# A weight ring of three places in place of four, and two and a half weight pieces kept

## The chip, the cores and the metric

One Trainium2 chip, one of its cores. The time is what the device takes for one execution, in microseconds (us), median of the runs shown; lower is better. All data is float32. A megabyte of weights (1024 KB) is one "piece" here, a tile of 128 partitions by 2048 values.

## The reference, cut to what matters

One inference step of a two-layer decoder trunk: 256 prompt tokens and 32 sample tokens (8 sequences of 4), width 1024. Per layer three mixers (a spatial-gating MLP, a gated causal convolution, and cross-attention into 256 memory tokens) share one input projection; then comes a retrieval of single-neuron experts, 8 heads of 16 out of 16384 per token.

```python
xn = _rmsnorm(x, w['norm_mix_g'])
h = xn @ w['w_in']                       # 1024 x 8192, columns split below
u_a, v_a, val_b, gate_b, q_m, gl_a, gl_b, gl_m = jnp.split(h, SPLITS, axis=-1)
y_a, vn = _spatial_gate(gelu(u_a), gelu(v_a), ...)
c = causal_depthwise(val_b * sigmoid(gate_b))
y_b = silu(layernorm(c))
y_m = _mem_attend(q_m, mem_k, mem_v)
merged = sigmoid(gl_a)*(y_a @ w_o_a) + sigmoid(gl_b)*(y_b @ w_o_b) + sigmoid(gl_m)*(y_m @ w_o_m)
x = x + merged @ w_out
# then the retrieval: top 16 of 16 x 16 product keys, per head
hid = gelu(einsum('bd,bhkd->bhk', xb, u_tab[eid]))
x = x + einsum('bhk,bhkd->bd', g * hid, v_tab[eid])
```

The "v half" of the title is v_a: its 1024 x 1024 weights come as four pieces, va 0 to va 3, of 256 columns each.

## The kernel before, in words

**Portions.** The work is cut into four portions. Portions 0 and 2 (even, layers 0 and 1) carry 128 prompt tokens; portions 1 and 3 (odd, same layers) carry the other 128 prompt tokens and the 32 sample tokens. Each portion has a mixing part (dense matmuls with streamed weights) and a retrieval part. The mixing of portion m + 1 runs woven into the retrieval of portion m; the mixing of portion 0 runs alone, at the start, with no gathers beside it.

**Retrieval.** A portion has 8 or 10 steps of 8 units t. A unit gathers 2 x 128 rows of 8 KB of the expert table: POOL issues two indirect DMAs of 1 MB each into one of 5 slots (`gather`, L560), DVE takes dot products with them (L1558), ACT scales (L944), and PE multiplies the value halves (`values`, L2294), which frees the slot (semaphore `v_used`). POOL issues the gather of unit t + 5 when unit t is through.

**Streamed weights.** `items(m)` lists the pieces in the order in which PE wants them. Even portions: glu 0 to 7, mk and q mixed, mv 0, q 3, mv 1 to 3, va 0 to 3, 24 pieces mg mixed with ua 0 to 3, out 0 to 3, wq 0 to 3. Odd portions: glu, q, va 0 to 2, ck 0 to 7 (the sample's cached keys), va 3, cv 0 to 7 (cached values), then as before. All of them that aren't kept elsewhere are numbered in `ITEMS` (L81). Item n goes into place n % RING of the ring; SP issues its load (`load`, L447; L436 for ck and cv) after a wait for PE's last use of item n - RING (`freed`). SP runs its whole program in order: a wait for a place also holds back everything written behind it, stores and other loads too. PE waits for the landing (`landed`) and takes each piece once.

```python
KEPT = [("va", 3)]
HALF_KEPT = ("va", 2)
ITEMS = [it for m in range(PORTIONS) for it in items(m) if it not in EARLY and it[1] != "keys" and it[1:] not in KEPT]
RING = 4
                n = ITEM[m, kind, i]
                if n >= RING:
                    name, k = freed(*ITEMS[n - RING])
                    sp.wait_ge(S[name], k)
                to = ring[n % RING]
```

**Kept pieces.** The odd portion of a layer uses the same weights as the even one. va 3 (`KEPT`) has a buffer of its own, is loaded in the even portion only (L427), and used in both. Of va 2 (`HALF_KEPT`) the first half is loaded once per layer into `kept_half` (L445) and the second half into a ring place in every portion (L440, 512 KB). va 3 is used in the odd portion behind the ck pieces; va 2 ahead of them.

**Other DMAs of SP's queue near the change's effects.** Right behind mv 0 of portion 0, SP issues four broadcast rows of 512 KB each (L497, L499) and the four pieces `EARLY` (glu 0 to 3 of portion 1, L502) into gather slots that are still empty. Behind out 0 of an even portion SP loads the stored memory values back (1 MB, L506). In an odd portion the stores convp_out and convs_out stand behind q 3, ahead of va 0. At the end of portion 0's mixing, `first_tail` on PE runs the first half-products of out 0, 1 and 2 before it finishes out 0 (and so frees its place); it takes out 3 after that, then wq 0 to 3.

Of the kernel before, what the change touches and what calls it, by code (L numbers as in the profile page):

```python
# [64 lines left out]
def items(m):  # L65
    if m % 2 == 0:
        kinds = [("glu", 0, 8), ("mk", 0, 1), ("q", 0, 1), ("mk", 1, 2), ("q", 1, 2), ("mk", 2, 3), ("q", 2, 3), ("mk", 3, 4),
                 ("mv", 0, 1), ("q", 3, 4), ("mv", 1, 4), ("va", 0, 4)]
    else:
        kinds = [("glu", 0, 8), ("q", 0, 4), ("va", 0, 3), ("ck", 0, 8), ("va", 3, 4), ("cv", 0, 8)]  # L70
    kinds += [("mg", 0, 8), ("ua", 0, 4), ("mg", 8, 24), ("out", 0, 4), ("wq", 0, 2), ("keys", 0, 1), ("wq", 2, 4)]
    return [(m, k, i) for k, a, b in kinds for i in range(a, b)]
# [2 lines left out]

EARLY = [(1, "glu", i) for i in range(4)]

KEPT = [("va", 3)]

HALF_KEPT = ("va", 2)  # L80
ITEMS = [it for m in range(PORTIONS) for it in items(m) if it not in EARLY and it[1] != "keys" and it[1:] not in KEPT]  # L81
ITEM = {it: n for n, it in enumerate(ITEMS)}
RING = 4
WKIND = [("glu", 8), ("mk", 4), ("mv", 4), ("q", 4), ("va", 4), ("ua", 4), ("mg", 24), ("mw", 24), ("out", 4), ("wq", 4)]


# [32 lines left out]
def freed(m, kind, i):  # L119

    name, k = {"glu": ("pe_glu", 2 * i + 2), "mk": ("pe_mk", i + 1), "mv": ("pe_mv", i + 1), "q": ("pe_q", i + 1),
               "ck": ("pe_sk", i + 1), "va": ("pe_va", i + 1), "cv": ("pe_so", i + 1), "mg": (("pe_mg", "pe_proj")[m % 2], i + 1),
               "ua": ("pe_ua", i + 1), "out": ("pe_out", i + 1), "wq": ("pe_wq", i + 1)}[kind]
    return name, at(name, m, k)
# [100 lines left out]
def build(nc, x_in, consts_in, mem_in, cache_in, state_in, w_in, small_in, vecs_in, fing_in, ws_in, wss_in,  # L225
          keys_in, uv_in, y_out, memk_out, memv_out, convp_out, convs_out, vn_out):
    with ExitStack() as ctx:
        def sb(name, shape, dt=F32):
            return ctx.enter_context(nc.sbuf_tensor(name, shape, dt))

        def sem(name):
            return ctx.enter_context(nc.semaphore(name))

        S = {name: sem("s_" + name) for name in tuple(PER) + RUN}
        w_landed = [sem(f"w_landed{i}") for i in range(RING)]
        uv_landed = [sem(f"uv_landed{i}") for i in range(SLOTS)]
        x_landed = [sem(f"x_landed{t}") for t in range(TILES)]
        early_landed = [sem(f"early_landed{i}") for i in range(len(EARLY))]
        kept_landed = [sem(f"kept_landed{i}") for i in range(len(KEPT))]
        row_landed, half_scored, first_read = sem("row_landed"), sem("half_scored"), sem("first_read")  # L240
# [14 lines left out]
        uvbuf = [uv_region[:, 2 * D * i:2 * D * (i + 1)] for i in range(2 * SLOTS)]  # L255
        ring_region = sb("ring", [P, RING * 2 * D])
        ring = [ring_region[:, 2 * D * i:2 * D * (i + 1)] for i in range(RING)]

        kept_region = sb("kept", [P, len(KEPT) * 2 * D])
        kept = [kept_region[:, 2 * D * i:2 * D * (i + 1)] for i in range(len(KEPT))]  # L260
        kept_half = sb("kept_half", [P, D])
# [121 lines left out]
        def landed(m, kind, i):  # L383
            if (m, kind, i) in EARLY:
                return early_landed[i], 16
            if (kind, i) in KEPT:
                return kept_landed[KEPT.index((kind, i))], 16 * (m // 2 + 1)
            if kind == "keys":
                return keys_landed, 16 * (m // 2 + 1)
            n = ITEM[m, kind, i]  # L390
            return w_landed[n % RING], 16 * (n // RING + 1)

# [9 lines left out]
        def buf(m, kind, i):  # L402
            if (m, kind, i) in EARLY:
                return uvbuf[6 + i]
            if (kind, i) in KEPT:
                return kept[KEPT.index((kind, i))]
            return ring[ITEM[m, kind, i] % RING]

        @block.sync
        def _(sp):  # L410
            def load(m, kind, i):
# [17 lines left out]
# [3 lines that stand above are left out]
# [5 lines left out]
                else:  # L437
                    r = NW * l + WROW["mw" if m % 2 == 0 and kind == "mg" else kind, i]
                    if (kind, i) == HALF_KEPT:
                        sp.dma_start(to[:, D:2 * D], w_in[P * r:P * (r + 1), D:2 * D]).then_inc(w_landed[n % RING], 16)  # L440
# [1232 lines left out]
        def _(pe):  # L1673
            MM = nc.tensor.matmul

            def weights(m, kind, i):
                pe.wait_ge(*landed(m, kind, i))
                return buf(m, kind, i).rearrange("p (k c) -> p k c", k=KB)
# [13 lines left out]
            def by_block(w):  # L1692
                return [w[:, k, :] for k in range(KB)]
# [22 lines left out]
            def mixing(m):  # L1716
# [22 lines left out]
                def bank_for(name):  # L1739

                    if TURN[p][name][1]:
                        of, k = emptied(m, name)
                        pe.wait_ge(S[of], k)
                    return dense(m, name)
# [88 lines left out]
                def va(i):  # L1833
                    yield place[f"va{i}"]
                    w, out = by_block(weights(m, "va", i)), bank_for(f"va{i}")
                    if ("va", i) == HALF_KEPT:
                        pe.wait_ge(kept_half_landed, 16 * (l + 1))
# [576 lines left out]
```

## Time and profile before

| | |
|---|---|
| median of 3 runs | 2240.13 us (2239.24 to 2240.17) |
| span of the profiled execution, first to last instruction | 2236.6 us |
| PE busy | 1631.0 us (73%) |
| DVE busy | 1582.1 us (71%) |
| DMA traffic | 895.56 MB, mean 400 GB/s |
| of it gathers (software queue) | 604.02 MB |
| of it loads and stores of SP's queue (hardware queue) | 289.54 MB |
| ring loads of 1 MB: w_in, cache_in | 211 and 32 |

The profiled execution has no time of its own beside its span; the span is 3.5 us below the median of the runs. The span begins with the first instruction, and windows are counted in us from there. PE, DVE, ACT and POOL are the computing engines, SP only issues DMAs. The gathers begin at 261 us and the last ends near 2228 us. GB/s is what the core's 16 DMA engines moved, all queues together; at 421 GB/s a piece takes 1.049 / 421 = 2.49 us.

### The profile page before, as it was taken

How to read it: one execution, taken by the hardware profiler on the slowest of the kernel's cores; microseconds unless marked ns; L12 is line 12 of the kernel's file. 1: busy time of each engine (PE TensorE's matmuls, PEld its weight loads, DVE VectorE, ACT ScalarE, POOL GpSimd, SP SyncE). 2: the span in 40 equal slices, each digit the busy share in tenths (PEclk: the TensorE clock that was granted, in tenths of full speed). 3: DMA queues.
4: the chain of work that ended last, by engine and by line, in shares of the span. 5: the costliest groups of instructions: out<-in, count | busy, mean ns of one | idle time of the engine just before them, and what ended most of it. 6: DMA issues, size and time to landing. Idle time of an engine off the chain costs nothing.

```text
span 2236.6 us, 31371 instructions
## 1 busy us (share of the span) xinstructions
PE 1631.0 (73%) x10944; PEld 1064.6 (48%) x10944; DVE 1582.1 (71%) x4234; ACT 658.9 (29%) x1649; POOL 673.1 (30%) x596
## 2 busy tenths in 40 slices
PE   9999988489897477878788647776999854334334
PEld 8965775258775055654434315543888620000002
DVE  3563498788856667787775568977876687776875
ACT  2112235231313242422132323342223323322222
POOL 0000132123222432332223243221323354454443
PEclk9999998689998588889789767876999875555556
DMA  8788999999999999999999999999999999999998
GB/s 310 292 299 291 366 420 411 411 420 420 421 420 418 421 421 421 417 396 422 421 377 422 421 421 420 421 397 400 405 421 420 414 398 421 422 421 421 421 421 334
DMA packets 127772, 895.56 MB, mean 400 GB/s; under 512 B 16096, under 2 KB 16928, under 8 KB 20480
## 3 DMA queue, kind: packets, MB, share of 16 engines
q0 software_dynamic: 83232, 604.02, 65.3%
q1 hardware_dynamic: 44384, 289.54, 32.4%
q8 instruction: 88, 1.44, 0.3%
q14 instruction: 68, 0.56, 0.1%
HBM read 885.39 MB, written 8.11 MB: 399 GB/s over the span
## 4 chain that ended last, share of the span: by engine, by line
PE 35%; DMA 33%; DVE 19%; ACT 4%; issue 4%; DVEq 3%; POOL 1%; SPq 0%; POOLq 0%; ACTq 0%
DMA uv<-uv_in,idx_u 24%; PE bank L1683 16%; DVE uv L1558 9%; DMA ring<-w_in 6%; PE bank L1959 5%; PE bank L2294 5%; PE bank L1689 4%; DMA ring<-cache_in 3%; DVE yB L1051 2%; ACT L612 1%; POOL uv L560 1%; DVE x L1581 1%; ACT diag L944 1%; DVEq L1046 1%; PE bank L2055 1%
## 5 line engine op out<-in xcount | busy, mean ns | idle before, releaser
L560 POOL DMA_INDIRECT uv<-uv_in,idx_u x574 | 656.9, 1144 | 1369.0 <-PE bank L2294 679.4
L1558 DVE CUSTOM_DVE_ANT_0 uv<-uv,xrep 128x1024 f32<-128x1024 f32 x576 | 681.2, 1220 | 217.3 <-DMA uv<-uv_in,idx_u 216.1
L2294 PE MATMUL bank<-uv,diag 128*32 128x512 f32 x2176 | 396.9, 810 | 450.9 <-ACT diag L944 447.8
L1683 PEld LDWEIGHTS bank<-xnT,ring 128*128 128x128 f32 x3168 | 428.6, 199 | 80.5 <-issue 64.9
L1683 PE MATMUL bank<-xnT,ring 128*128 128x160 f32 (+1 forms) x3168 | 450.2, 302 | 5.8 <-DMA ring<-w_in 5.8
L612 ACT ACTIVATE pick<-pick 128x2 f32<-128x2 f32 (+1 forms) x315 | 66.9, 212 | 1055.5 <-DVE pick L1558 1055.0
L2294 PEld LDWEIGHTS bank<-uv,diag 128*32 128x32 f32 x2176 | 50.3, 122 | 637.1 <-ACT diag L944 572.8
L1051 DVE SCALAR_TENSOR_TENSOR yB<-ext_p,small,yB 128x128 f32<-128x128 f32 x960 | 276.6, 350 | 20.7 <-issue 1.3
L612 ACT ACT_TABLE_LOAD x139 | 178.3, 1283 | 2.4
L944 ACT ACTIVATE diag<-gated_fold,pick 128x32 f32<-128x32 f32 x574 | 153.1, 314 | 9.7 <-ACT pick L612 0.3
L1959 PE MATMUL bank<-ring,xnT 128*128 128x512 f32 x192 | 86.9, 607 | 0.0
L1683 PE MATMUL bank<-yMA,ring 128*128 128x160 f32 x512 | 74.1, 299 | 0.0
L612 ACT ACTIVATE phase<-bank 128x512 f32<-128x512 f32 (+2 forms) x44 | 23.2, 528 | 162.8 <-PE bank L1683 66.3
L1683 PEld LDWEIGHTS bank<-yMA,ring 128*128 128x128 f32 x512 | 71.1, 190 | 0.0
L928 ACT ACTIVATE xrep<-xnf 32x1024 f32<-32x1024 f32 x64 | 67.4, 1053 | 1.5
L1689 PE MATMUL bank<-ring,ext_s 128*128 128x256 f32 x256 | 62.0, 405 | 0.0
L612 ACT ACTIVATE sg<-bank 128x160 f32<-128x160 f32 (+1 forms) x80 | 23.5, 294 | 124.9 <-PE bank L1683 124.7
L1959 PEld LDWEIGHTS bank<-ring,xnT 128*128 128x128 f32 x192 | 36.6, 194 | 45.9 <-issue 45.6
L2287 PE MATMUL bank<-uv,diag 128*32 128x256 f32 x256 | 27.7, 572 | 41.6 <-ACT diag L944 41.0
L1689 PEld LDWEIGHTS bank<-ring,ext_s 128*128 128x128 f32 x256 | 52.2, 206 | 12.2 <-issue 4.2
L1959 PE MATMUL bank<-ring,yMA 128*128 128x512 f32 x128 | 58.0, 607 | 0.0
L1683 PE MATMUL bank<-ext_s,ring 128*128 128x256 f32 x256 | 57.0, 381 | 0.0
(301 smaller groups left out, 1820.9 us busy)
## 6 DMA issues: line engine op xcount, KB each, us to landing
ring<-w_in SPq DMA_DIRECT2D x211, 1024.0 KB, 9.9
ring<-cache_in SPq DMA_DIRECT2D x32, 1024.0 KB, 16.7
uv<-uv_in,idx_u POOLq DMA_INDIRECT x578, 16.7
uv<-w_in SPq DMA_DIRECT2D x4, 1024.0 KB, 16.5
ring<-w_in SPq DMA_DIRECT2D x6, 512.0 KB, 8.1
ext_s<-state_in SPq DMA_DIRECT2D x2, 1088.0 KB, 17.2
convs_out<-ext_s SPq DMA_DIRECT2D x2, 1088.0 KB, 27.9
ext_s<-mem_in SPq DMA_DIRECT2D x2, 1024.0 KB, 15.3
```

The costliest lines, as they stand in the source:

```text
L560: nc.gpsimd.indirect_dma_start(out=uvbuf[2 * b + i], out_offset=None, in_=uv_in, in_offset=bass.IndirectOffsetOnAxis(ap=ids[:, c:c + 1], a ...
L612: ins = nc.scalar.activation(out, in_, func, bias=bias, scale=scale, **({} if accum is None else {"accum_out": accum}))
L928: ins = nc.scalar.activation(xrep[gg % 2][32 * i:32 * (i + 1), :], xnf[1 if t == 2 else 0][r0:r0 + 32], ACT.Copy)
L944: ins = nc.scalar.activation(diag[:, t % 4, i], gated_fold[:, c], ACT.Copy, scale=gel[:, 16 * (s % 2) + c:16 * (s % 2) + c + 1])
L1046: dve.drain()
L1051: ins = V.scalar_tensor_tensor(out=yB[:, c, 0:P], in0=ext_p[:, c, w:w + P], scalar=wconv[:, c, w:w + 1], in1=yB[:, c, 0:P], op0=ALU.mult, ...
L1558: ins = V.tensor_tensor_reduce(out=u, in0=u, in1=xrep[gg % 2][:, :], scale=1.0, scalar=0.0, op0=ALU.mult, op1=ALU.add, accum_out=hid[:, c: ...
L1683: ins = MM(out, w[:, k, P * b:P * (b + 1)], rhs(k), start=k == 0, stop=k == KB - 1)
L1689: ins = MM(out, lhs(k), w[k], start=k == 0, stop=k == KB - 1)
L1959: ins = MM(out[:, :], rows[:, 4 * (i % 2) + k, 0:P], w[:, k, :], start=i % 2 == 0 and k == 0, stop=i % 2 == 1 and k == 3)
L2287: ins = MM(vbank[gg % 2][32 * q:32 * (q + 1), 0:256], diag[:, t % 4, i], uvbuf[2 * b + i][:, c:c + 256], start=first and i == 0, stop=last ...
L2294: ins = MM(vbank[gg % 2][c:c + 32, :], diag[:, t % 4, i], uvbuf[2 * b + i][:, D + 512 * n:D + 512 * (n + 1)], start=first, stop=last)
```

## The change: three places in the ring, and the freed megabyte keeps weights

Three constants change; the code that reads them does the rest.

```diff
-KEPT = [("va", 3)]
-
-HALF_KEPT = ("va", 2)
+KEPT = [("va", 2), ("va", 3)]
+
+HALF_KEPT = ("va", 1)
 ITEMS = [it for m in range(PORTIONS) for it in items(m) if it not in EARLY and it[1] != "keys" and it[1:] not in KEPT]
 ITEM = {it: n for n, it in enumerate(ITEMS)}
-RING = 4
+RING = 3
```

The ring is 1 MB smaller and the `kept` region 1 MB larger, so the memory used is the same. va 2 and va 3 have buffers of their own, loaded in portions 0 and 2 (in portion 2 after a wait for portion 1's last use). Of va 1 the first half is in `kept_half` and the second half goes through the ring in every portion. va 2 is out of `ITEMS`, so each portion has one item less.

## Rows read from the trace of the kernel before

**Rows 1.** The page: span, engines, memory traffic in 40 slices, ring loads

```profile
span 2236.6 us, 31371 instructions
...
PE 1631.0 (73%) x10944; PEld 1064.6 (48%) x10944; DVE 1582.1 (71%) x4234; ACT 658.9 (29%) x1649; POOL 673.1 (30%) x596
...
GB/s 310 292 299 291 366 420 411 411 420 420 421 420 418 421 421 421 417 396 422 421 377 422 421 421 420 421 397 400 405 421 420 414 398 421 422 421 421 421 421 334
DMA packets 127772, 895.56 MB, mean 400 GB/s; under 512 B 16096, under 2 KB 16928, under 8 KB 20480
...
ring<-w_in SPq DMA_DIRECT2D x211, 1024.0 KB, 9.9
```

**Rows 2.** Windows: stretch, length, engines' busy us, PEclk, DMA share, GB/s

```profile
0.00:261.00 261.00, 255.68 (x1377) 197.40 (x1378) 124.98 (x385) 56.54 (x107) 3.09 (x8) 1.00 0.82 305
970.00:1000.00 30.00, 24.26 (x114) 15.98 (x114) 28.11 (x78) 7.75 (x24) 11.37 (x9) 0.83 0.95 378
1120.00:1170.00 50.00, 43.28 (x152) 20.11 (x149) 38.25 (x97) 14.94 (x28) 12.60 (x12) 0.89 0.96 371
1460.00:1480.00 20.00, 17.78 (x246) 12.82 (x238) 14.50 (x43) 12.44 (x33) 8.54 (x8) 0.97 0.94 360
1550.00:1580.00 30.00, 27.53 (x183) 22.86 (x184) 19.45 (x53) 6.73 (x18) 6.72 (x6) 0.82 0.90 351
1780.00:1810.00 30.00, 23.83 (x236) 16.22 (x239) 21.00 (x60) 11.97 (x36) 13.93 (x12) 0.94 0.95 366
1810.00:2200.00 390.00, 150.29 (x756) 20.68 (x748) 291.12 (x712) 114.75 (x310) 184.66 (x154) 0.51 1.01 421
```

**Rows 3.** Timeline of SP's queue, 62 to 70 us: start, length, issues

```profile
62.79 0.33 SPq L447 DMA_DIRECT2D ring<-w_in  x1
63.16 1.69 SPq L497 DMA_DIRECT2D uv<-vecs_in  x3
...
65.38 2.00 SPq L502 DMA_DIRECT2D uv<-w_in  x4
69.70 0.33 SPq L447 DMA_DIRECT2D ring<-w_in  x1
```

**Rows 4.** DMA issues, us to landing; issued at 62.8, 69.7, 142.5, 152.8, 207.1 us

```profile
ring<-w_in SPq DMA_DIRECT2D x1, 1024.0 KB, 4.7
...
ring<-w_in SPq DMA_DIRECT2D x1, 1024.0 KB, 19.1
...
ring<-w_in SPq DMA_DIRECT2D x1, 1024.0 KB, 7.3
...
ring<-w_in SPq DMA_DIRECT2D x1, 1024.0 KB, 7.5
...
ring<-w_in SPq DMA_DIRECT2D x1, 1024.0 KB, 7.8
```

**Rows 5.** Timeline of PE, 81 to 98 us

```profile
82.16 7.07 PE L1689 MATMUL bank<-ring,ext_s 128*128 128x256 f32 x32
89.06 3.73 PE L1683 MATMUL bank<-xnT,ring 128*128 128x128 f32 x32
```

**Rows 6.** Chain of waits, 190 to 232 us: start, length

```profile
196.80 30.90 PE bank L1959 x72
```

**Rows 7.** Timeline of PE, 222 to 300 us

```profile
231.41 3.62 PE L2055 MATMUL bank<-ring,yMA 128*128 128x256 f32 x16
...
235.30 7.07 PE L2055 MATMUL bank<-ring,yMA 128*128 128x256 f32 x32
...
242.65 3.62 PE L2055 MATMUL bank<-ring,yMA 128*128 128x256 f32 x16
```

**Rows 8.** DMA issues, us to landing; issued at 238.9 us

```profile
ring<-w_in SPq DMA_DIRECT2D x1, 1024.0 KB, 4.8
```

**Rows 9.** DMA issues, us to landing; issued at 1394.1 us

```profile
ring<-w_in SPq DMA_DIRECT2D x1, 1024.0 KB, 15.3
```

**Rows 10.** Timeline of PE, 1400 to 1480 us

```profile
1452.67 6.56 PE L1689 MATMUL bank<-ring,xnT 128*128 128x256 f32 x16 [12.43 <-DMA ring<-w_in]
```

## The prediction

> **What bounds the kernel now.** First the page [rows 1]: no engine fills the span (PE 73%), but the line of memory traffic has two regimes. In the first four slices it is near 300 GB/s, and from slice 5 on it stands at 420 or 421 with a few dips. Then the windows [rows 2]: up to 261 us PE is busy 255.7 of 261.0 us at full clock with 305 GB/s moved, so portion 0's mixing is bound by PE and the memory has room; from 1810 to 2200 us PE is busy 150 of 390 us at 421 GB/s, so there the transfers bind, and they do so nearly everywhere behind 261 us. The dips are where both queues ran dry. In the five stretches shown the traffic missing against 421 GB/s is 30 x 43/421 = 3.1 us, 50 x 50/421 = 5.9, 20 x 61/421 = 2.9, 30 x 70/421 = 5.0 and 30 x 55/421 = 3.9 us: 20.8 us together. So two different prices hold: ahead of 261 us each microsecond that PE waits for a weight piece is a microsecond of the total, and nothing behind gives it back, since the transfers that bind later can't begin sooner than the first expert ids. Behind 261 us the price is bytes, and a late piece costs only where it opens a dip.
>
> **The bytes removed.** An odd portion no longer loads the half of va 2 (512 KB) nor half of va 1: 1 MB less in portion 1, 1 MB less in portion 3. Even portions load what they did: va 2 whole into its own buffer, va 1 in two halves. 2 x 1.049 MB at 421 GB/s [rows 2] is **-5.0 us**, all of it in the stretch that transfers bind. The two DMA issues fewer on SP and its waits cost nothing either way, SP idles most of the time.
>
> **The ring of three.** A load of item n now waits for item n - 3 instead of n - 4. In the old trace that is the instant at which item n + 1 was issued. So I read the landing of each piece in the new kernel from the old landing of the piece behind it, and hold it against the old time of use. From issue to use there are now two pieces of PE's work in place of three.
>
> *First pieces.* The ring starts with three pieces in place of four, but the queue behind them is full (memory tokens and x rows), so glu 3 and the next ones land in the same order and at the same time. Nothing.
>
> *mv 0 and q 3 of portion 0.* This is the largest term. mv 0 was issued at 62.79 us and landed 4.7 us later; SP issued the broadcast rows and the four early pieces right behind it, and then, at 69.70 us, q 3, which landed after 19.1 us, at 88.8 [rows 3, 4]. PE took q 3 at 89.06 us, with no more than 0.3 us to spare [rows 5]. From mv 0's landing (67.5) to q 3's (88.8) the queue works off 7 MB without a pause: 21.3 us. With three places mv 0 has to wait for the place that freed at 69.70. It lands at 69.7 + 4.7 = 74.4, and its own use at 82.16 [rows 5] is safe; but the 6 MB between it and q 3 stand behind SP's wait, and q 3 lands at 74.4 + 21.3 = 95.7. PE waits 95.7 - 89.06 plus 0.1 for the semaphore: **+6.8 us**. What is queued behind it on PE (all of portion 0) moves with it; the next pieces, mv 1 and mv 2, follow q 3 at 2.5 us each and PE needs 7 us for one, so they add nothing.
>
> *mg, ua and again mg of portion 0.* PE takes 30.90 / 9 = 3.43 us for a piece [rows 6]. Issue to use shrinks from 10.3 to 6.87 us. A load alone takes 4.7 or 4.8 us [rows 4, 8], which still fits by 2 us. Some take longer: 7.3, 7.5 and 7.8 us for those issued at 142.5, 152.8 and 207.1 us [rows 4]. These come 0.4, 0.6 and 0.9 us late, each plus 0.1: 2.2 us, a little less where one wait spares the next. I take **+2.0 us**, bounds 0 (the slow loads fall elsewhere) and 3.
> By the Trainium skill (DMA: Bandwidth & Descriptors, Anatomy of one DMA) a transfer takes about 2.0 us plus its bytes at 436 GB/s, an estimate of 4.4 us for a piece, and two pieces of cover would never be short; with it this term would be nothing and the total 2 us lower. The rows that show 7.3 to 7.8 us speak against it.
>
> *The tail of portion 0.* PE takes out 0 at 231.41 us, out 1 half a row of 3.45 us later, at 233.1, and out 3 at 242.65 [rows 7]. The place for out 1 now frees about when PE ends the last mg pieces (227.7), and its load stands behind out 0's, issued 224.3, and the 1 MB of memory values: 224.3 + 4.8 + 2 x 2.5 = 234.1. That is 1.0 us late, more if it is one of the slow ones. out 2 follows at its time or up to 1.7 us late. out 3 used to be there; its place is now out 0's, which frees at 238.9, and a load issued at that instant took 4.8 us [rows 8]: 243.7 + 0.1 against 242.65, 1.2 us. Sum **+3.0 us**, bounds 2.2 and 4.8. wq 0 to 3 shift with it and keep a margin.
>
> Up to 261 us: 6.8 + 2.0 + 3.0 = 11.8 us, bounds 9 and 14.6. PE was busy 98% there, so there is no idle time to eat it up, and the first gather starts that much later.
>
> **Behind 261 us** PE and the weights are more often late, which is paid only in dips. Three kinds of place. In odd portions, where PE works in bursts, glu 7 to q 3 of portion 3 are read from the old row: q 0 took 15.3 us from 1394.1 [rows 9], with the stored keys' load ahead of it; one piece later in the same queue, at half the bandwidth (2 x 2.5 = 5 us), it comes 4 us late. va 0 behind the stores already kept PE idle 12.43 us, until 1452.67 [rows 10], and the dip at 1460 us follows it [rows 2]; it lands up to 5 us later, so this dip may grow by 1 to 3 us. Among the cached keys the place of ck 3 frees only with ck 0, since va 2 no longer passes through: one stage of PE's work later, in stretches that the gathers fill at 421 GB/s. The last mg pieces of portions 1 to 3 come late by up to one piece, 5 us. Where transfers bind, three outstanding loads keep the hardware queue as full as four: a ring load takes 9.9 us in the median [rows 1], two pieces' time at half the bandwidth. Bounds: -1 (less queued ahead of ck 0) and +10 (each of the five dips grows by 2). I take **+2.5 us**, near the lower end, since the waits name no ring load for PE around the dips at 970, 1120 and 1780 us; only those at 1460 and 1550 follow one.
>
> **Sum** against the profiled execution: 2236.6 + 11.8 - 5.0 + 2.5 = 2245.9 us span, and with the 3.5 us that the median of the runs lies above the span, 2249.4 us, 0.4% slower.
>
> **Rivals.**
> *Faster by the bytes.* The other side: the removed 2 MB count fully (-5.0 us) and the first portion's loss stays under them. It needs q 3 to land within about 3 us of its old time. The place is the 6 MB of early loads: if the queue had been idle between them the shift by 6.9 us would be swallowed. 6 MB at 2.5 us each need 15 us out of the 21.3, so at most some 6 us of slowness could be elastic. For it speaks that broadcast rows of 4 KB may be slow for reasons that a later start avoids; against it that SP's issues lie back to back [rows 3] and that the landing followed them without a pause. It would give 2240.1 + 1 + 2 - 5 = 2238 or less, down to 2235. The point from which it decides is a first-portion loss below 4 us. Chance 6% (2231 to 2235.6).
> *A draw.* First portion +8, bytes -5, no new dips: 2243; or the first portion +5: 2240. Chance 15%.
> *Dips grow.* The woven portions lose 7 to 10 us instead of 2.5, because a late piece holds the values of later units and with them POOL's next gathers: 2240.1 + 11.8 - 5 + 10 = 2257. For it: POOL has only five slots, and both waits for the ring are already followed by a dip [rows 2, 10]. Against: most of the woven stretches stand at 420 to 421 GB/s [rows 1], where a late piece costs nothing. Chance 18%.
> *The change doesn't remove what it says.* If va 2 were still loaded in odd portions, bytes would stay: 2254. The item list excludes it for every portion, so 1%.
> The forecast, 2244.7 to 2254, has the remaining 60%.
>
> **How the numbers follow.** About 0.2%, 4.5 us, is what a measurement of this kernel can tell from no change: 2235.6 to 2244.6 is "same". Faster 6%, same 15%, slower 60 + 18 + 1 = 79%. The predicted time is the forecast's. Range 2241 to 2258: the sum of the lower bounds is 2240.1 + 9 - 5 - 1 = 2243, widened by 2 toward the draw, and the upper end takes in most of the grown dips.
>
> **What would show it.** PE's timeline near 89 us with an idle time of 6 to 7 us put down to a ring load, the first gather near 272 us instead of 261, ring loads of w_in fewer by about four whole ones, 893.5 MB in all, PE waiting about 1 us before out 3, traffic at 421 GB/s as before behind that, and dips of some 23 to 30 us. The prediction is wrong if q 3 arrives within 3 us of its old time, if the first gather moves by less than 9 us, or if the dips behind 272 us sum to more than 32 us.

## The result and the profile after

The changed kernel is slower: 2272.01 us (median of 4 runs, 2268.39 to 2276.07) against 2239.68 us (median of 4, 2238.37 to 2240.17), a ratio of 1.0144 with a 95% interval of 1.0132 to 1.0156. That is +32.3 us where +9.3 was forecast. The profiled execution took 2274.15 us, 1.9 us of it outside its span.

The page of the kernel after, the lines that answer to [rows 1]:

```profile
span 2272.2 us, 31369 instructions
...
PE 1638.4 (72%) x10944; PEld 1072.1 (47%) x10944; DVE 1581.6 (70%) x4234; ACT 659.6 (29%) x1649; POOL 672.5 (30%) x596
...
GB/s 271 275 281 289 326 405 372 395 367 419 419 421 420 420 421 418 421 415 419 421 378 422 421 421 403 420 345 410 397 420 421 417 408 421 422 422 421 421 421 326
DMA packets 127485, 893.46 MB, mean 393 GB/s; under 512 B 16065, under 2 KB 16897, under 8 KB 20449
...
ring<-w_in SPq DMA_DIRECT2D x207, 1024.0 KB
...
kept<-w_in SPq DMA_DIRECT2D x4, 1024.0 KB, 13.0
```

The bytes went as the change says: 895.56 - 893.46 = 2.10 MB less, four ring pieces fewer. No engine has more work worth the difference (PE +7.4 us). What changed is the traffic line: lower in the first four slices, then 372, 395 and 367 in slices 7 to 9, and 345 in slice 27.

Where the time went, in windows (columns as in [rows 2]). The kernel after:

```profile
0.00:370.00 370.00, 343.51 (x2008) 269.71 (x2008) 207.91 (x618) 93.33 (x193) 35.55 (x38) 0.97 0.83 316
370.00:520.00 150.00, 93.09 (x870) 58.28 (x870) 104.69 (x311) 43.46 (x107) 33.30 (x32) 0.73 0.93 372
520.00:1380.00 860.00, 654.34 (x4053) 424.21 (x4052) 608.75 (x1604) 250.85 (x645) 275.99 (x246) 0.85 1.01 417
1380.00:1610.00 230.00, 165.49 (x1349) 115.84 (x1350) 175.97 (x491) 80.31 (x188) 55.99 (x53) 0.78 0.96 389
1610.00:2200.00 590.00, 348.90 (x2391) 188.45 (x2394) 440.05 (x1125) 172.59 (x464) 246.85 (x208) 0.69 1.01 419
```

The same windows of the kernel before:

```profile
0.00:370.00 370.00, 344.98 (x2103) 270.06 (x2104) 216.38 (x641) 95.78 (x199) 35.78 (x39) 0.98 0.88 338
370.00:520.00 150.00, 111.06 (x983) 74.26 (x982) 119.56 (x342) 48.01 (x122) 42.29 (x40) 0.82 1.00 413
520.00:1380.00 860.00, 647.64 (x3970) 413.88 (x3969) 609.22 (x1606) 259.26 (x658) 273.27 (x246) 0.83 1.01 416
1380.00:1610.00 230.00, 177.98 (x1477) 130.15 (x1475) 183.18 (x516) 70.24 (x177) 60.59 (x54) 0.83 0.99 406
1610.00:2200.00 590.00, 328.50 (x2244) 164.49 (x2240) 435.13 (x1097) 177.93 (x470) 249.00 (x208) 0.66 1.01 418
```

A stretch's loss is the bytes it moved too few, at 421 GB/s: 370 x (338 - 316)/421 = **19.3 us** up to 370 us, 150 x (413 - 372)/421 = **14.6** up to 520, then -2.0, then 230 x (406 - 389)/421 = **9.3** from 1380 to 1610, then -1.4. Together 39.8; less the 5.0 us of bytes not moved this is 34.8 of the 35.6 us by which the spans differ. Of the 19.3, 14.6 are the first gather, which starts at 275.63 instead of 261.08 us; the other 4.7 follow it. GB/s are whole numbers here, so a term is good to about 0.5 us where the window is 370 us long and to 1 us where it is 860. So the change costs time in two places, portion 0 and the first 250 us or so of each odd portion's mixing, and hardly anywhere else.

**Portion 0.** The timeline of PE after:

```profile
20.55 3.84 PE L1683 MATMUL bank<-xnT,ring 128*128 128x128 f32 x32 [0.43 <-DMA ring<-w_in]
27.93 5.34 PE L1683 MATMUL bank<-xnT,ring 128*128 128x128 f32 x32 [3.54 <-DMA ring<-w_in]
...
97.39 6.39 PE L1683 MATMUL bank<-xnT,ring 128*128 128x128 f32 x32 [4.68 <-DMA ring<-w_in]
...
245.92 1.99 PE L2055 MATMUL bank<-ring,yMA 128*128 128x256 f32 x8 [1.64 <-DMA ring<-w_in]
...
257.09 3.72 PE L2055 MATMUL bank<-ring,yMA 128*128 128x256 f32 x16 [1.11 <-DMA ring<-w_in]
```

and the kernel before at its only wait there:

```profile
25.95 3.84 PE L1683 MATMUL bank<-xnT,ring 128*128 128x128 f32 x32 [1.98 <-DMA ring<-w_in]
```

The last line of before ends at 29.79 us and the second of after at 33.27: +3.5 in the first pieces. q 3 ends at 103.78 where it ended at 92.79 [rows 5]: +11.0, so +7.5 at q 3. The rest, 14.6 - 11.0 = +3.6, lies in the tail, at out 1 and out 3. The mg and ua loads between them made no wait. Of the 3.5 us, 1.5 are slower matmuls (5.34 us for 3.84), and so are 2.7 of the 7.5 at q 3 (6.39 for 3.73); the last section comes back to them.

**Portion 1.** The timeline of SP after (start, length, issues):

```profile
318.73 0.33 SPq L447 DMA_DIRECT2D ring<-w_in  x1
319.17 0.38 SPq L481 DMA_DIRECT2D phase<-memk_out  x1
323.07 24.00 SPq L447 DMA_DIRECT2D ring<-w_in  x4
347.12 0.63 SPq L486 DMA_DIRECT2D convp_out<-ext_p  x1
347.80 1.37 SPq L488 DMA_DIRECT2D convs_out<-ext_s  x1
353.15 0.33 SPq L447 DMA_DIRECT2D ring<-w_in  x1
```

and before:

```profile
268.93 0.33 SPq L481 DMA_DIRECT2D phase<-memk_out  x1
303.16 15.76 SPq L447 DMA_DIRECT2D ring<-w_in  x4
...
329.24 0.66 SPq L488 DMA_DIRECT2D convs_out<-ext_s  x1
329.94 4.99 SPq L447 DMA_DIRECT2D ring<-w_in  x2
```

The stored keys (memk_out) used to be asked for at 269 us, right at the start of portion 1. It stands behind glu 7, whose place used to be that of the last wq piece of portion 0 (four items back); three items back is glu 4 of portion 1 itself, and PE ends that only near 319 us. So the keys go out at 319, and q 0 behind them comes late. q 3's place is free only when q 0 is through (346.7), and the two stores stand behind q 3's wait; va 0 stands behind the stores, and its own place frees at 353.1. PE after:

```profile
339.23 7.49 PE L1683 MATMUL bank<-xnT,ring 128*128 128x160 f32 x32 [4.11 <-DMA ring<-w_in]
...
385.30 4.91 PE L1689 MATMUL bank<-ring,xnT 128*128 128x256 f32 x12 [15.03 <-DMA ring<-w_in]
...
1488.89 5.25 PE L1689 MATMUL bank<-ring,xnT 128*128 128x256 f32 x16 [17.73 <-DMA ring<-w_in]
```

and before, where the wait in portion 3 is that of [rows 10]:

```profile
361.28 5.05 PE L1689 MATMUL bank<-ring,xnT 128*128 128x256 f32 x11 [6.06 <-DMA ring<-w_in]
```

va 0 reaches PE 24.0 us later than before, 9.4 us more than the shift of the first gather. The landing itself is as long as it was; the chain of waits has it behind va 0's issue, after

```profile
353.15 32.11 DMA ring<-w_in
```

and before:

```profile
329.94 31.30 DMA ring<-w_in
```

So it is the issue that came later. Against the shift of 14.6 us the stores go out 4.0 us later (347.12 for 328.56) and va 0 8.7 us later (353.15, right after PE's use of q 1 frees its place, for 329.94). While PE stands still it multiplies no values, so no gather slot comes free. POOL's timeline after:

```profile
370.71 1.28 POOL L560 DMA_INDIRECT uv<-uv_in,idx_u  x1 [0.30 <-issue]
393.77 0.94 POOL L560 DMA_INDIRECT uv<-uv_in,idx_u  x1 [21.79 <-PE bank L2294]
```

Before, the longest such gap here was 12.62 us. The gathers already issued run out, the traffic falls to 238 GB/s, and that is part of the lost traffic of the second window:

```profile
380.00:395.00 15.00, 9.70 (x103) 7.49 (x104) 0.00 (x0) 0.89 (x3) 0.94 (x1) 0.68 0.60 238
```

### The profile page after: what moved, and what is told of

Read it like the earlier page. It is cut to its first block, busy times and chain, and to the rows that moved or that the text cites. A ratio compares the mean times of both kernels' runs of the same rounds, so it can differ in the third digit from the quotient of the medians.

```text
span 2272.2 us, 31369 instructions
## 1 busy us (share of the span) xinstructions
PE 1638.4 (72%) x10944; PEld 1072.1 (47%) x10944; DVE 1581.6 (70%) x4234; ACT 659.6 (29%) x1649; POOL 672.5 (30%) x596
## 2 busy tenths in 40 slices
DMA packets 127485, 893.46 MB, mean 393 GB/s; under 512 B 16065, under 2 KB 16897, under 8 KB 20449
## 4 chain that ended last, share of the span: by engine, by line
PE 36%; DMA 33%; DVE 18%; issue 4%; ACT 4%; DVEq 3%; POOL 1%; SPq 0%; POOLq 0%; ACTq 0%
DMA uv<-uv_in,idx_u 19%; PE bank L1683 17%; DMA ring<-w_in 10%; DVE uv L1558 8%; PE bank L1959 5%; PE bank L2294 5%; PE bank L1689 4%; DMA ring<-cache_in 3%; DVE yB L1051 2%; POOL uv L560 1%; ACT L612 1%; DVE x L1581 1%; ACT diag L944 1%; DVEq L1046 1%; DMA ext_s<-mem_in 1%
## 5 line engine op out<-in xcount | busy, mean ns | idle before, releaser
L1683 PEld LDWEIGHTS bank<-xnT,ring 128*128 128x128 f32 x3168 | 437.8, 203 | 101.0 <-issue 57.9
L1683 PE MATMUL bank<-xnT,ring 128*128 128x160 f32 (+1 forms) x3168 | 460.2, 306 | 25.5 <-DMA ring<-w_in 25.5
L612 ACT ACTIVATE yMA<-bank 128x256 f32<-128x256 f32 (+2 forms) x54 | 22.2, 411 | 161.0 <-PE bank L1683 91.4
```

Of the source, the lines that this page charges most:

```text
L612: ins = nc.scalar.activation(out, in_, func, bias=bias, scale=scale, **({} if accum is None else {"accum_out": accum}))
L1683: ins = MM(out, w[:, k, P * b:P * (b + 1)], rhs(k), start=k == 0, stop=k == KB - 1)
```

## The experiments

Twelve kernels, all computing the whole result. Times are in us; the kernel before was timed on the same chip as each.

| label | median (range, runs) | kernel before | ratio, 95% |
|---|---|---|---|
| e1_ring3_only | 2277.72 (2272.08 to 2282.41, 4) | 2239.67 | 1.0166 (1.0145 to 1.0188) |
| e5_no_half | 2242.83 (2240.66 to 2244.22, 10) | 2239.67 | 1.0013 (1.0004 to 1.0023) |
| e3_keys_early | 2269.84 (2263.72 to 2272.73, 4) | 2239.67 | 1.0125 (1.0108 to 1.0142) |
| e4_early_late | 2263.96 (2259.13 to 2264.95, 4) | 2239.67 | 1.0101 (1.0085 to 1.0118) |
| e7_stores_late | 2260.21 (2250.34 to 2263.97, 4) | 2239.76 | 1.0081 (1.0053 to 1.0108) |
| e8_all_three | 2249.37 (2246.91 to 2250.98, 5) | 2239.76 | 1.0041 (1.0027 to 1.0055) |
| e6_stores_late_before | 2240.74 (2238.48 to 2242.36, 10) | 2239.76 | 1.0001 (0.9992 to 1.0011) |
| e9_all_four | 2239.45 (2238.26 to 2242.19, 10) | 2239.76 | 1.0001 (0.9991 to 1.0010) |
| e10_three_in_0 | 2252.82 (2250.97 to 2254.47, 4) | 2240.10 | 1.0061 (1.0044 to 1.0078) |
| e11_three_in_odd | 2258.25 (2253.80 to 2261.54, 4) | 2240.10 | 1.0080 (1.0062 to 1.0098) |
| e12_three_in_2 | 2240.50 (2237.09 to 2243.14, 10) | 2240.10 | 0.9998 (0.9988 to 1.0008) |
| e13_early_and_stores | 2249.66 (2247.58 to 2252.43, 4) | 2240.10 | 1.0049 (1.0032 to 1.0065) |

### The ring and the bytes apart

The kernel before with the smaller ring alone:

```diff
-RING = 4
+RING = 3
```

> Three places, but the kept pieces as before (va 3 whole, va 2 half). If the whole loss comes from the ring's waits and the removed 2 MB are worth their bytes, this is 5 us slower than the changed kernel: about 2277 us, 37 above the kernel before, and the first portion ends 14.6 us late as in the changed kernel. If it is the kept pieces that hurt (their loads' places in SP's order, va 2 no longer passing through the ring ahead of the cached keys), this is faster than the changed kernel, 2262 or less.

It gave 2277.7, +38.0. The changed kernel differs from it only by the kept pieces, and it is 5.7 us faster, near the 5.0 that the bytes should give. The ranges of the two overlap, and so do their intervals, so I priced the bytes once more, at four places, by keeping less instead of more:

```diff
-HALF_KEPT = ("va", 2)
+HALF_KEPT = ("none", 0)
```

> The kernel before with four places, and nothing kept of va 2: each odd portion loads 512 KB more, through the ring. Theory: behind 261 us bytes cost what 421 GB/s makes of them, 2 x 0.524 MB = 2.5 us: 2242.4. Rival: the kept half gains nothing, or more than its bytes (then the price by bytes is wrong): within 0.5 us of 2240, or above 2245.

1.05 MB more cost 3.2 us (interval 0.9 to 5.2), where 421 GB/s make 2.5. Both agree with the price by bytes, if loosely, and the smaller ring alone has the whole loss.

### Which portion pays

The kernel before, with the wait of the smaller ring in some portions only; for e11 the condition is `m % 2 == 1`, for e12 `m == 2`:

```diff
-                    name, k = freed(*ITEMS[n - RING])
+                    name, k = freed(*ITEMS[n - (3 if m == 0 else RING)])
```

> The kernel before, four places and its own kept pieces, but in portion 0 every load also waits for the use of the item three ahead of it, as a ring of three would. If a late piece of portion 0 is paid in full and given back nowhere, this is 14.6 us slower than before (3.5 at glu 3 and 4, 7.5 at q 3, 3.6 in the tail): 2254. If what follows gives some back: 2250 or less.

> The same wait on the item three ahead, in portions 1 and 3 only. The kernel with three places and the old kept pieces is 38 us slower than before; with 14.6 of it in portion 0, the odd portions should hold nearly all of the other 23: 2260 to 2264. Rival: the loss is spread over portions 1 to 3 or comes from the change of phase between PE and the gathers that portion 0's delay makes: 2252 or less.

> The same in portion 2 only, where the late pieces (mg 17 to 23, out) lie in a stretch that the gathers fill at 421 GB/s: 0 to 3 us, 2240 to 2243.

Portion 0 costs 12.7 us, the odd portions 18.2, portion 2 nothing that can be measured. e11 lies between its two expectations, 2 us below the first and 6 above the rival; its wait for va 0 in portion 1 is 13.77 us with no delay of portion 0 ahead of it, so the late stores and va 0 don't need that delay. In e10 the first gather came at 271.18, 10.1 us later than in the profile of before, and the window from 520 to 1380 moved 417 GB/s; nothing behind gave the loss back. e10 misses its expectation by 2 us, and PE's timeline shows where a part of it may lie:

```profile
25.01 3.84 PE L1683 MATMUL bank<-xnT,ring 128*128 128x128 f32 x32 [1.41 <-DMA ring<-w_in]
...
93.27 5.26 PE L1683 MATMUL bank<-xnT,ring 128*128 128x128 f32 x32 [4.99 <-DMA ring<-w_in]
```

q 3's wait is there, that of the first pieces is not. The edit leaves the first fill at four pieces (`if n >= RING` with RING = 4), so glu 3 was not held, nor was what is written behind it. In the changed kernel it is; SP's timeline after,

```profile
3.71 9.63 SPq L447 DMA_DIRECT2D ring<-w_in  x3
13.37 0.43 SPq L469 DMA_DIRECT2D ext_s<-mem_in  x1
```

and before:

```profile
3.84 1.40 SPq L447 DMA_DIRECT2D ring<-w_in  x3
5.28 0.49 SPq L469 DMA_DIRECT2D ext_s<-mem_in  x1
```

The third of those pieces waits, and the memory tokens and the x rows go out 8 us later, just ahead of glu 4. The parts sum to 31.3 us against 38.0 for the whole. Up to 3.5 of the missing 6.7 us may be this first fill; the rest was not settled. The 6.7 us themselves are not clear of the noise: by their intervals e1 costs 32 to 42 us, e10 10 to 17 and e11 14 to 22, and single runs of one three-place kernel lie 4 to 14 us apart.

### What stands behind SP's wait

Each of the next edits is made on the changed kernel and moves something out from behind a wait for a place. First the stored keys, one item earlier in portions 1 and 3:

```diff
-                    if p == 1 and n == 8:
+                    if p == 1 and n == 7:
```

> The changed kernel with the load of the stored memory keys (phase<-memk_out) moved one item forward in the odd portions, ahead of glu 7's wait for a place. Theory: in portion 1 that 1 MB waited until 319 us behind glu 7's place, so that q 0, q 3, the two stores and va 0 came late, one after the other. Then PE's wait before q 0 of portion 1 (4.1 us) goes, va 0 comes 7 to 9 us sooner, and the time falls by 6 to 9 us, to about 2264. Rival: what opens the dips between 380 and 510 us is the shallower ring itself, and this changes the time by less than 2 us.

Only 2.2 us, which is a miss and not clear of the noise. The edit did what it says: in its profile the keys are asked for at 287.7 and q 0 starts without a wait. The stores went out at 345.4 and 346.0, which is 0.5 us late once the later first gather of this profile (by 16.3 us) is taken off. But va 0 still stood behind them, and its place was free only behind q 1 (issued 349.7), and so

```profile
382.48 6.03 PE L1689 MATMUL bank<-ring,xnT 128*128 128x256 f32 x16 [8.85 <-DMA ring<-w_in]
```

va 0 still came 8.85 us late, and in portion 3 by 17.70, as before the edit. Against the first gather va 0 came 4.9 us late in place of 9.4, so the keys were about half of portion 1's delay, and the window from 370 to 520 moves 384 GB/s in place of 372. What makes va 0's landing long, with three places and with four, the next edit shows.

Then the two stores behind va 1 in place of q 3:

```diff
-                    if p == 1 and (kind, i) == ("q", 3):
+                    if p == 1 and (kind, i) == ("va", 1):
```

> The changed kernel with the two convolution stores of the odd portions moved from behind q 3 to behind the half of va 1, so that va 0 no longer lands behind them. Theory: PE's waits before va 0 (15.0 us in portion 1, 17.7 us in portion 3) empty the five gather slots and open the dips around 390 and 490 to 1500 us; without them most of 14 us of dips go: 10 to 14 us off, 2258 to 2262. Rival: the stores are needed on time (the cached queries are spread only after them), so the wait moves to the cached keys and the time falls by less than 3 us.

-11.8 us, as expected. The load of va 0, issued at 354.4, was there by 371.9, in 17.5 us at most in place of 32. va 0 now follows q 3 with no wait at all in either odd portion, though q 0 still comes 4.31 us late:

```profile
340.82 7.14 PE L1683 MATMUL bank<-xnT,ring 128*128 128x160 f32 x32 [4.31 <-DMA ring<-w_in]
...
371.91 4.31 PE L1689 MATMUL bank<-ring,xnT 128*128 128x256 f32 x16
```

and the window from 370 to 520 moves 405 GB/s in place of 372:

```profile
370.00:520.00 150.00, 102.26 (x952) 65.96 (x948) 115.44 (x336) 46.58 (x118) 38.40 (x36) 0.78 0.99 405
```

Not all of the wait is gone. The list of waits of e7 (total us, times, longest):

```profile
PE bank L1851 <- DMA ring<-cache_in: 44.6, 15, 7.8
...
PE bank L1874 <- DMA ring<-cache_in: 21.1, 9, 4.5
```

The same two lines of the kernel after read 33.4 and 13.6: the stores now stand ahead of the cached keys. The traffic shows that it costs little there.

In portion 0, the four early pieces from behind mv 0 to behind mv 3 (the broadcast rows stay):

```diff
+                    if m == 0 and (kind, i) == ("mv", 3):
                         for _, _, c in EARLY:
```

> The changed kernel with the four pieces that are loaded early for portion 1 issued behind mv 3 in place of behind mv 0 (the broadcast rows stay). Theory: q 3 of portion 0 waits only for these 4 MB; PE's 4.7 us of waiting at 97 us go, and with them the 2.7 us by which the matmuls just behind the wait are slower: portion 0 ends 7.5 us sooner and the whole gains that, 2264.5. Rival: the early pieces compete with mv and va pieces instead, or the later phases take the gain back, so less than 3 us.

-8.0 us, as expected, and in PE's timeline the wait for q 3 is gone, the rest of portion 0 as it was:

```profile
92.98 3.73 PE L1684 MATMUL bank<-xnT,ring 128*128 128x128 f32 x32
```

The edits of e4 and e7 together:

> The changed kernel with two of the moves, early pieces behind mv 3 and stores behind va 1. If the two losses are separate places, the gains of the single moves add up: 2272.0 - 8.0 - 11.8 = 2252. If they are one loss seen twice, about 2260.

2249.7, 22.4 us below the changed kernel; singly they gave 8.0 and 11.8. So the two don't get in each other's way, and joined they give back two thirds of the loss of 32.3 us. One kernel moves all four things, the memory tokens and x rows ahead of glu 3 and the keys in both portions too:

```diff
-                    if p == 0 and n == 4:
+                    if p == 0 and n == (3 if m == 0 else 4):
...
-                    if p == 1 and n == 8:
+                    if p == 1 and n == (7 if m == 1 else 3):
...
-                    if p == 1 and (kind, i) == ("q", 3):
+                    if p == 1 and (kind, i) == ("va", 1):
...
+                    if m == 0 and (kind, i) == ("mv", 3):
                         for _, _, c in EARLY:
```

> The changed kernel with all of SP's order mended for three places: memory tokens and x rows ahead of glu 3 in portion 0, the early pieces behind mv 3, the stored keys ahead of the first item that waits for a place in the odd portions, the stores behind va 1. If the loss is what stands behind SP's waits for a place, and not the number of pieces in flight, it all goes except the tail of portion 0 (3.6 us) and the 5 us of bytes are left: 2238 to 2245. If the shallower ring itself starves PE behind 261 us, 2252 or more.

2249.4, the same as e13 within the ranges: the two further moves bring nothing that can be measured. It lies between its two expectations: the order of SP's program is the larger part of the loss and not all of it. Its first gather is at 267.25, 6.2 us later than before; the windows from 370 and 1380 move 398 and 401 GB/s against 413 and 406. What is left after the order is mended is 9.6 us, with the bytes already counted in, so with them taken out the ring of three still costs some 14.6 us. Waits for the shallower ring are still there (e13: 3.44 us at the first pieces, 1.65 and 0.99 at out 1 and out 3), and smaller dips; it wasn't taken apart further.

### Two of the moves at four places

The kernel before with the edit of e7 alone (e6), and with the keys of portion 3 moved as well (e9). The early pieces of portion 0 were not moved at four places.

```diff
-                    if p == 1 and n == 8:
+                    if p == 1 and n == (8 if m == 1 else 4):
```

> The kernel before (four places) with the same move of the two stores behind va 1. The same wait before va 0 is there, 6.1 and 12.4 us, and dips of 1.1 and 2.9 us follow it. If those dips are all that it costs, 2236 to 2238; if the stores then come too late for the cached keys, 2240 or more.

> As the last one, and in portion 3 the stored keys' load goes ahead of glu 4's wait for a place (in portion 1 it stays). It takes 1 MB out of the queue in front of q 0 of portion 3: 0 to 2 us less than the stores' move alone.

No difference in either. In e6 PE's wait before va 0 falls from 18.5 to 0.9 us over both portions, and the waits for cached keys and values rise from 34.6 and 15.7 to 37.0 and 20.0; the traffic from 370 to 520 us rises from 413 to 420 GB/s and from 1380 to 1610 from 406 to 412, but from 1610 to 1850 it falls from 414 to 410. The dips move. e6 came out at its second expectation, and neither kernel was measurably better than the kernel before.

## Why the prediction was wrong

The direction and the place of the first loss were right; the size was 23 us short.

- **The bytes removed**, -5.0: right, as far as the intervals of e1 and e5 can tell.
- **mv 0 and q 3**, +6.8: right in mechanism and nearly in size. It measured +7.5 and e4 gets 8.0 back. But the nearness is in part luck. The wait was only 4.68 us: q 3 landed at 97.35, 24.2 us after mv 0's issue at 73.2, where the prediction added up 26.0 (69.7 to 95.7). The late first pieces don't explain it, since they moved mv 0's issue by as much as PE; e10, without them, waits 4.99 us. The other 2.7 us of the term are q 3's own matmuls, 6.39 us in place of 3.73, at a lowered clock (below), for which the prediction had no term.
- **First pieces**, "Nothing": wrong, up to +3.5. I took the queue behind the third piece to be the same. It was held: SP stood at glu 3's wait with the memory tokens and x rows behind it. How much of the 3.5 is due to this is not shown. e8 puts them back ahead of glu 3 and ends these matmuls at 32.11 us; e13 leaves them behind and ends at 31.51. And this wait scatters with four places too: 1.34 to 3.18 us in the seven profiles with a first fill of four pieces, in one of them with 6.57 us of matmuls behind it, against 3.30 to 3.72 us in the six with three pieces and the same order. The end of these matmuls scatters accordingly, 28.9 to 33.8 us with a first fill of four and 31.5 to 34.2 in those six, and the shift of the first gather by 14.6 us is good to a few us for the same reason.
- **mg, ua and again mg**, +2.0: 0. The slow loads of [rows 4] did not come back: PE waited for none of these pieces. By the landings in the trace all took 4.7 to 5.8 us but one, of 7.4, whose piece PE took only later. The rule of the Trainium skill that the prediction weighed there (DMA: Bandwidth & Descriptors, Anatomy of one DMA) made this term nothing, and here the trace agrees that it was nothing. The page gives this fit for the GpSimd path, though, and these loads go by SP's queue, where a lone piece takes 4.7 to 4.9 us; by the page's figures it would be an estimate of 4.4.
- **The tail of portion 0**, +3.0: +3.6, right, at out 1 and out 3 as named.
- **Up to 261 us**: 14.6 us against 11.8, right at the upper bound (14.6).
- **Behind 261 us**, "I take +2.5 us", bounds -1 and +10: this is the step that failed. It measured 4.7 + 14.6 - 2.0 + 9.3 - 1.4, some 25 us. The prediction took va 0 of portion 3 to land up to 5 us later, and had no term of its own for va 0 of portion 1, where the largest of the losses behind 370 us lies. The rival that dips grow had the right mechanism (a late piece holds the values and with them POOL's gathers) at less than half of the size. Of the prediction's own signs those on the first gather, the bytes, the four ring loads and out 3 came as said; the one on the dips, 23 to 30 us in all, did not: the 20.8 us of before grew by some 25.

Within that step the mistake has two parts. First, I read the landing of each piece as that of the piece behind it, and so one piece (5 us) later at most. That holds where nothing but pieces is in SP's program. Where a load or a store of another kind is written between two pieces, it shifts too, and it can shift by much more: the keys by 50 us (36 in e11, where portion 0 isn't late), since the place ahead of them now came from portion 1's own work and not from the end of portion 0's. Second, I took q 0's delay and va 0's as two separate ones, each within cover. They are linked: q 0 late, so its place late, so q 3's issue late, so the stores late by 4.0 us, of which e3, with q 0 on time, has 0.5 left. va 0 then waits for q 1's use as well, and was issued 8.7 us late (3.4 in e3), into a landing of 31 to 32 us behind the stores that was already too long with four places. PE's wait grew by 9.0 us in portion 1 and 5.3 in portion 3. The price of a wait in this stretch was also higher than thought: 9.0 us more of waiting at va 0 and 4.1 at q 0 went with 14.6 us less traffic. That the wait for va 0 is behind it e7 shows, where the wait is gone and 11.8 of the 14.6 us come back. How much of the price is the stop of POOL's gathers and how much PE's lower clock was not taken apart.

The Trainium skill has the first half of this (DMA: Bandwidth & Descriptors, Anatomy of one DMA): a semaphore wait of a DMA happens on the issuing sequencer before dispatch, and the DMA engines just work off their queues. The SP timelines agree: the load of the keys, which waits for no place of its own, went out 50 us later. The prediction used this for the 6 MB in portion 0 and not for the loads and stores of portions 1 and 3.

What stays open: the difference between e1 and the sum of e10 to e12 beyond the first fill, some 3 us and within the noise, and how the leftover 9.6 us of e8 and e13 divides behind 370 us.

## What to carry to other kernels

When a ring loses a place, list not the pieces but everything that the issuing engine's program has between two waits, and read for each entry when the wait ahead of it will now end; a load or store without a place of its own can lose its whole lead. Follow the delay on to the next place it frees: a late use is a late issue one ring further. Look for loads whose landing is long, too, here that of va 0 behind the stores: with them a later issue is a later use. Two moves in SP's order gave back two thirds of the loss with three places. One of them, that of the stores, was worth 11.8 us there and nothing with four places, so the order of a queue and the depth of its ring are to be judged together. The megabyte that the smaller ring sets free saved some 5 us of transfers, and the place that it took from the ring was worth 38.

## What was not expected of the hardware

PE's clock falls within the waits that a late piece makes, and the matmuls behind pay. Windows of the kernel after around q 3 (after the five engines: PEclk, DMA share, GB/s):

```profile
88.00:92.00 4.00, 4.00 (x20) 3.52 (x19) 0.72 (x3) 0.00 (x0) 0.00 (x0) 1.00 1.01 428
92.00:97.00 5.00, 0.71 (x4) 0.28 (x2) 2.85 (x11) 1.05 (x3) 0.00 (x0) 0.90 1.01 424
97.00:99.00 2.00, 1.61 (x7) 1.61 (x8) 1.09 (x4) 0.00 (x0) 0.00 (x0) 0.50 1.02 426
99.00:101.00 2.00, 2.00 (x12) 2.00 (x11) 0.00 (x0) 0.00 (x0) 0.00 (x0) 0.50 1.01 422
...
103.50:110.00 6.50, 6.50 (x38) 5.88 (x37) 2.86 (x10) 1.04 (x3) 0.00 (x0) 1.00 0.53 195
```

PE was busy at full clock until its wait began, and came out of it at 0.50, the 1.2 GHz level, while most of q 3's matmuls ran; later it is back at 2.4 GHz. Thus a wait of 4.68 us cost 4.68 + 2.7 us. The same after the wait of 3.54 us at 27.93 (5.34 for 3.84, with 0.50 granted from 28 to 30 us) and of 4.11 us at 339.23 (7.49 us; the same 32 matmuls take 4.51 to 4.61 in the next groups). It doesn't follow from the wait's length alone: in e13 a wait of 3.44 us at the first pieces was followed by matmuls of the usual 3.84 us, and in e6 one of 3.18 by 5.36. The Trainium skill (TensorE: Matmul & The Clock Gate, the part on the clock gate) says that the low level is the default and that activity releases it; the rows agree: 0.50 behind the wait, 1.00 once PE has worked again.
